# Gated scores in 32x32 tiles, keys times values in 64 columns, and finer waits, in a two-layer hybrid trunk

## The reference, cut to what matters

```
u = rms_norm(h) @ w_in            # split among four mixers
SSD and retention, 4 heads of 64: S_t = a_t S_{t-1} + k_t^T v_t,  o_t = q_t S_t       (a_t a scalar per head)
GLA, 4 heads, keys of 32:         S_t = diag(exp(g_t)) S_{t-1} + k_t^T v_t, o_t = q_t S_t
RG-LRU:                           h_t = a_t h_{t-1} + u_t, with gates sigmoid(x @ w_a), sigmoid(x @ w_x)
h += concat(y_ssd, y_ret, y_gla, y_lru) @ w_out
h += (silu(rms_norm(h) @ w_gate) * (rms_norm(h) @ w_up)) @ w_down     # 2816 wide
```

## Time and profile before

| what | value |
|---|---|
| median of 3 runs | 1399.87 us (1399.63 to 1401.17) |
| profiled execution | 1401.04 us |
| its span | 1399.0 us |
| PE busy | 1369.9 us, 98% of the span |
| PE weight loads | 1320.2 us, 94% |
| VectorE busy | 638.1 us, 46% |
| ScalarE busy | 492.9 us, 35% |
| GpSimd busy | 409.6 us, 29% |

### The profile page before, as it was taken

The page is one execution under the profiler, slowest core; times in us unless marked ns, Lnnn a source line. Parts: engine busy times, 40 slices in busy tenths (PEclk is TensorE's granted clock), DMA queues, the critical chain, the costliest instruction groups (busy, mean ns, idle before and its releaser), DMA issues.

```text
span 1399.0 us, 25881 instructions
## 1 busy us (share of the span) xinstructions
PE 1369.9 (98%) x11245; PEld 1320.2 (94%) x11245; DVE 638.1 (46%) x1234; ACT 492.9 (35%) x675; POOL 409.6 (29%) x204
## 2 busy tenths in 40 slices
PE   7999999999999999999999999999999999999996
PEld 7888888999999999999998798899999999999996
DVE  5844775553321443133657456646433123422434
ACT  6525354432221222122553364543322122222231
POOL 1100001434334443344400000024344334443341
PEclk9999999999999999999999999999999999999998
DMA  7745644222332223322466565422322232223321
GB/s 246 180 107 137 159 95 110 86 78 89 92 91 86 82 90 91 91 83 84 131 139 154 120 153 120 103 88 84 89 82 88 91 91 86 83 90 91 91 91 64
DMA packets 42065, 147.05 MB, mean 105 GB/s; under 512 B 5216, under 2 KB 6496, under 8 KB 41952
## 3 DMA queue, kind: packets, MB, share of 16 engines
q1 hardware_dynamic: 30672, 111.95, 25.4%
q0 software_dynamic: 6624, 24.12, 10.5%
q10 hardware_dynamic: 4656, 9.34, 2.1%
HBM read 137.34 MB, written 5.82 MB: 102 GB/s over the span
## 4 chain that ended last, share of the span: by engine, by line
PE 86%; DVE 8%; DVEq 2%; ACT 2%; issue 1%; DMA 1%; SPq 0%; ACTq 0%
PE bank L1264 77%; DVE ct L754 1%; PE bank L1212 1%; DVE lru_x L754 1%; PE bank L1394 1%; PE bank L1420 1%; PE bank L1509 1%; PE bank L1228 0%; DMA h<-x 0%; DVEq L753 0%; PE bank L1515 0%; PE bank L1223 0%; DVE sq_sum L688 0%; PE bank L1445 0%; DVE h L1203 0%
## 5 line engine op out<-in xcount | busy, mean ns | idle before, releaser
L1264 PE MATMUL bank<-xh,wh 128*128 128x272 f32 x2208 | 649.2, 294 | 8.0 <-DVE xl L709 7.7
L1264 PE MATMUL bank<-xh,wl 128*128 128x272 f32 x2208 | 641.5, 291 | 0.0
L1264 PE MATMUL bank<-xl,wh 128*128 128x272 f32 x2208 | 637.6, 289 | 0.0
L390 POOL TENSOR_TENSOR wl<-raw,wh 128x1024 fp32r<-128x1024 f32 x154 | 369.4, 2399 | 591.7 <-ACT wh L419 572.4
L1264 PEld LDWEIGHTS bank<-xh,wh 128*128 128x128 f32 x2208 | 418.4, 189 | 15.7 <-issue 13.4
L419 ACT ACTIVATE wh<-raw 128x1024 fp32r<-128x1024 f32 x199 | 210.2, 1056 | 611.4 <-PE bank L1264 611.4
L1264 PEld LDWEIGHTS bank<-xl,wh 128*128 128x128 f32 x2208 | 418.9, 190 | 1.4 <-issue 1.0
L1264 PEld LDWEIGHTS bank<-xh,wl 128*128 128x128 f32 x2208 | 417.7, 189 | 0.0
L1181 DVE TENSOR_TENSOR tz<-bank,rs_bcast 128x272 f32<-128x272 f32 x176 | 77.5, 442 | 293.3 <-PE bank L1264 289.3
L1161 DVE TENSOR_TENSOR h<-h,bank 128x272 f32<-128x272 f32 x128 | 55.4, 436 | 217.3 <-PE bank L1264 217.2
L396 POOL DMA_DIRECT2D wl<-weights x46 | 39.9, 868 | 371.7 <-ACT wl L418 371.7
(11 more groups left out here) (361 smaller groups left out, 1750.6 us busy)
## 6 DMA issues: line engine op xcount, KB each, us to landing
raw<-weights SPq DMA_DIRECT2D x202, 512.0 KB, 3.6
wl<-weights POOLq DMA_DIRECT2D x46, 512.0 KB, 6.9
h<-x SPq DMA_DIRECT2D x4, 544.0 KB, 6.0
y<-h SPq DMA_DIRECT2D x4, 544.0 KB, 2.7
rv<-rk ACTq DMA_DIRECT2D x8, 136.0 KB, 7.0
tz<-rq ACTq DMA_DIRECT2D x8, 136.0 KB, 4.6
S<-s_ssd ACTq DMA_DIRECT2D x2, 512.0 KB, 7.0
n_ssd<-Vx ACTq DMA_DIRECT2D x2, 512.0 KB, 3.2
```

The costliest lines, as they stand in the source:

```text
L390: nc.gpsimd.tensor_tensor(wl[:, s, :], raw[:, s, :], wh[:, s, :].bitcast(F32), ALU.subtract).then_inc(lo_done, 1)
L1264: ins = mm(bank_, wt[:, n % RING, w], xx[:, cols], start=(i == 0 and j == 0), stop=(i == len(ks) - 1 and j == 2))
```

## The change

Four things are changed; all else stays.

1. GLA's scores: `kz` and the product that filled it are gone. Each matmul takes 32 key rows of one head and 32 stationary columns (tile position (32 hd, 32 j)); head hd writes bank M[0], M[2], M[3] or M[4], and the order goes through diagonals, so that four neighbours differ in rows and columns. VectorE masks with four products. Since M[3] is now written here, `gla_a_` waits for `gla_s` of the chunk before, as `gla_b_` did.
2. Keys times values in SSD, GLA and retention: one matmul per group (per head in retention) with 64 stationary columns and only the values that belong to it. The states shrink from 256 to 128 columns, and so do the three state outputs.
3. `lru_gates`: the four matmuls into M[4] wait for the convolution alone, the gates of t = 0 for a new signal `ssd_read` (M[0] and M[1] read), those of t = 1 for `ssd_s`.
4. Order: in `ssd_a_` the decay matrix comes first, then transposes, scores and the 64-row decays last; in `ret_a_` all transposes come ahead of the scores.

```diff
+GLA_BANKS = (0, 2, 3, 4)
...
-        kz = sb("kz", [4, P])
+        st_stacks = sb("st_stacks", [4, P])
...
-        S_ssd, S_gla, S_ret = sb("S_ssd", [256]), sb("S_gla", [256]), sb("S_ret", [256])
+        S_ssd, S_gla, S_ret = sb("S_ssd", [P]), sb("S_gla", [P]), sb("S_ret", [P])
...
                     if c == SAMPLE:
-                        dve.drain()
+                        dve.drain().then_inc(ssd_read.sem, 1)
                         for r in range(2):
                             tt(S1[:, 512 * r:512 * r + 512], S1[:, 512 * r:512 * r + 512], M[2 + r][:], ALU.add)
                     else:
                         if c == 0:
-                            copy(S_ssd[:], M[2][:, 0:256])
+                            copy(S_ssd[:], M[2][:, 0:P])
...
-                    if c < SAMPLE:
-                        tt(kz[:], ge[:, 0, :].unsqueeze(1).to_broadcast([P, 4, n]), per_head(cst("gla_heads"), P, n),
-                           ALU.mult)
-                    else:
+                    if c == SAMPLE:
...
-                    tt(PT, M[0][:].rearrange("p (h i) -> p h i", h=4), cst("keep").unsqueeze(1).to_broadcast([n, 4, n]),
-                       ALU.mult)
+                    for hd in range(4):
+                        tt(PT[:, hd, :], M[GLA_BANKS[hd]][:, 0:n], cst("keep"), ALU.mult)
                     dve.drain().then_inc(gla_bin.sem, 1)
...
-                    for r in range(2):
-                        for g in range(2):
-                            mm(M[1][64 * g:64 * g + 64, r * P:r * P + P],
-                               exact("cum_head", P, 2 * g + r, 1).to_broadcast([P, 64]).bitcast(F32), cum.bitcast(F32), start=True, stop=True)
...
+                    for t in range(2):
+                        turn(M[2][:, P * (t + 1):P * (t + 2)], xbc[:, t, off:off + n])
+                    turn(M[1][:, 384:512], xbc[:, 2, off:off + n])
                     for g in range(2):
                         rows = slice(64 * g, 64 * g + 64)
                         mm(M[2 + g][:, 0:n], xbc[rows, 2, off:off + n], xbc[rows, 3, off:off + n], start=True, stop=True)
-                    for t in range(2):
-                        turn(M[2][:, P * (t + 1):P * (t + 2)], xbc[:, t, off:off + n])
-                    turn(M[1][:, 384:512], xbc[:, 2, off:off + n]).then_inc(ssd_a.sem, 1)
+                    for r in range(2):
+                        for g in range(2):
+                            ins = mm(M[1][64 * g:64 * g + 64, r * P:r * P + P],
+                               exact("cum_head", P, 2 * g + r, 1).to_broadcast([P, 64]).bitcast(F32), cum.bitcast(F32), start=True, stop=True)
+                    ins.then_inc(ssd_a.sem, 1)
...
-                    mm(M[2][:, 0:256], K[:, 0:P], Vd[:], start=True, stop=True).then_inc(ssd_b.sem, 1)
+                    for g in range(2):
+                        ins = mm(M[2][64 * g:64 * g + 64, 0:P], K[:, 64 * g:64 * g + 64], Vd[:, P * g:P * g + P],
+                                 start=True, stop=True)
+                    ins.then_inc(ssd_b.sem, 1)
...
                     pe.wait_ge(conv_done.sem, conv_done.at(layer, 6))
-                    pe.wait_ge(ssd_s.sem, ssd_s.at(layer, 5))
...
                     for t in range(2):
+                        if t == 0:
+                            pe.wait_ge(ssd_read.sem, ssd_read.at(layer, 1))
+                        else:
+                            pe.wait_ge(ssd_s.sem, ssd_s.at(layer, 5))
                         for i in range(2):
                             ins = mm(M[2 * t + i][:], gate(t, i), lru_x[:, t, 0:SEQ], start=True, stop=True)
                         ins.then_inc(lru_mm.sem, 1)
...
                         pe.wait_ge(gla_o.sem, gla_o.at(layer, c))
+                        pe.wait_ge(gla_s.sem, gla_s.at(layer, c))
...
-                    for hd in range(4):
-                        for j in range(4):
-                            mm(M[0][32 * j:32 * j + 32, hd * P:(hd + 1) * P], kz[:, hd, 32 * j:32 * j + 32],
-                               D[:, j, :], start=True, stop=True)
+                    for d in range(4):
+                        for hd in range(4):
+                            j, rows = (hd + d) % 4, slice(32 * hd, 32 * hd + 32)
+                            mm(M[GLA_BANKS[hd]][32 * j:32 * j + 32, 0:P], ge[rows, 0, 32 * j:32 * j + 32],
+                               D[rows, j, :], start=True, stop=True, tile_position=(32 * hd, 32 * j))
...
-                    mm(M[3][:, 0:256], K[:, 0:P], V[:], start=True, stop=True).then_inc(gla_b.sem, 1)
+                    for t in range(2):
+                        ins = mm(M[3][64 * t:64 * t + 64, 0:P], K[:, 64 * t:64 * t + 64], V[:, P * t:P * t + P],
+                                 start=True, stop=True)
+                    ins.then_inc(gla_b.sem, 1)
...
-                    for t in range(2):
-                        ins = mm(M[0][:, t * P:(t + 1) * P], K[:, t * P:(t + 1) * P], V[:, t * P:(t + 1) * P],
-                                 start=True, stop=True)
+                    for hd in range(4):
+                        t, e = hd // 2, hd % 2
+                        cols = slice(64 * hd, 64 * hd + 64)
+                        ins = mm(M[0][64 * e:64 * e + 64, 64 * t:64 * t + 64], K[:, cols], V[:, cols], start=True, stop=True)
                     ins.then_inc(ret_b.sem, 1)
```

More of the change, by code:

```diff
@@ L222, in trunk @@
         st_vx, st_wide = Vx[:, 1024:1536], Vx[:, 1536:2048]
-        st_k, st_q, st_kl, st_a = kz[:, 0, :], kz[:, 1, :], kz[:, 2, :], kz[:, 3, :]
+        st_k, st_q, st_kl, st_a = (st_stacks[:, i, :] for i in range(4))
         st_p, st_v, st_d, st_o = PT[:, 0, 0:NS], V[:, 0:64], V[:, 64:64 + NS], V[:, P:P + 64]
@@ L997, in gla_b_ @@
                     else:
-                        new = M[3][:, 0:256]
+                        new = M[3][:, 0:P]
                         if c == 0:
@@ L1057, in ret_b_ @@
                         for t in range(2):
[L1058 removed]
+                            cols = slice(64 * t, 64 * t + 64)
                             if c == 0:
@@ L1442, in gla_b_ @@
                         rows = slice(32 * hd, 32 * hd + 32)
-                        mm(M[2 - t][64 * e:64 * e + 64, 0:P], S_gla[rows, 64 * hd:64 * hd + 64],
+                        mm(M[2 - t][64 * e:64 * e + 64, 0:P], S_gla[rows, 64 * e:64 * e + 64],
                            qt[rows, (c + 1) % 2, 0, :], start=False, stop=True, tile_position=(32 * hd, 64 * e))
-                    mm(M[3][:, 0:256], K[:, 0:P], V[:], start=True, stop=True).then_inc(gla_b.sem, 1)
+                    for t in range(2):
+                        ins = mm(M[3][64 * t:64 * t + 64, 0:P], K[:, 64 * t:64 * t + 64], V[:, P * t:P * t + P],
+                                 start=True, stop=True)
+                    ins.then_inc(gla_b.sem, 1)
                 def ret_a_(c):
@@ L1468, in ret_a_ @@
                     for t in range(2):
+                        turn(M[3][:, 256 + t * P:256 + (t + 1) * P], rv[:, t, off:off + n])
+                    for t in range(2):
                         for e in range(2):
                             rows = slice(64 * e, 64 * e + 64)
-                            mm(M[e][0:n, t * P:t * P + n], rk[rows, t, off:off + n], rq[rows, t, off:off + n],
-                               start=True, stop=True)
-                    for t in range(2):
-                        ins = turn(M[3][:, 256 + t * P:256 + (t + 1) * P], rv[:, t, off:off + n])
+                            ins = mm(M[e][0:n, t * P:t * P + n], rk[rows, t, off:off + n], rq[rows, t, off:off + n],
+                                     start=True, stop=True)
                     ins.then_inc(ret_a.sem, 1)
@@ L1493, in ret_b_ @@
                         rows = slice(64 * e, 64 * e + 64)
-                        mm(M[3][64 * e:64 * e + 64, t * P:(t + 1) * P], S_ret[rows, 64 * hd:64 * hd + 64],
+                        mm(M[3][64 * e:64 * e + 64, t * P:(t + 1) * P], S_ret[rows, 64 * t:64 * t + 64],
                            qt[rows, c % 2, t, :], start=False, stop=True, skip_group_check=True)
-                    for t in range(2):
-                        ins = mm(M[0][:, t * P:(t + 1) * P], K[:, t * P:(t + 1) * P], V[:, t * P:(t + 1) * P],
-                                 start=True, stop=True)
+                    for hd in range(4):
+                        t, e = hd // 2, hd % 2
+                        cols = slice(64 * hd, 64 * hd + 64)
+                        ins = mm(M[0][64 * e:64 * e + 64, 64 * t:64 * t + 64], K[:, cols], V[:, cols], start=True, stop=True)
                     ins.then_inc(ret_b.sem, 1)
@@ L1800 @@
     conv_p, conv_s = conv[:, None, 0:3], conv[:, 3:].reshape(DEPTH, NSEQ, 3, 6 * P)
[L1801 to L1806 removed]
+    o_ssd = r["o_ssd"].reshape(DEPTH, 2, 64, 2, 64)
+    o_ret = r["o_ret"].reshape(DEPTH, 2, 64, 2, 64)
+    o_gla = r["o_gla"].reshape(DEPTH, 4, 32, 2, 64)
+    p_ssd = np.stack([o_ssd[:, h // 2, :, h % 2] for h in range(4)], axis=1)[:, None]
```

(2 more changed lines are left out.)

19 lines of the change are left out of this document (6 added, 13 removed).

## The result

The median after is 1394.21 us (1392.69 to 1401.40, 7 runs), beside 1400.82 us (1399.41 to 1406.38, 7 runs) of the kernel before on the same chip. The ratio is 0.9948, 95% interval 0.9923 to 0.9973. The profiled execution took 1394.02 us with a span of 1392.0 us, 7.0 us less than the one before. The kernel is faster, but the gain is half of the 13.1 us that were forecast: 6.6 by the medians, 8.8 once the time at the low clock is taken out. The median lies 0.3 us inside the upper end of the range.

A forecast was written before the change was run, and what follows sets the result against it. TensorE (PE) was taken to bound the kernel, with 86% of the chain. Savings of 4.2 + 1.6 + 1.0 + 1.2 + 3.0 + 1.7 + 0.4 = 13.1 from 1401.04 gave 1387.9 us, range 1383 to 1394.5.

The forecast's parts named there:

- Scores: GLA's scores in 32x32 tiles: 0.48 us instead of 1.01 per group, eight groups, 4.2 us saved, bounds 0 to 5.6.
- The first rival: GLA's scores: issue sets the pace, so the sixteen tiles gain nothing or little, 1392.1 us; chance 0.15.
- take turns: Slower rival at GLA's scores: the array does one record at a time, 3.5 us a group, 1412 us; chance 0.03.
- Keys times values: 64-column products: 1.6 us saved in SSD and GLA, bounds -0.6 to 3; 1.0 in retention, bounds 0 to 2.
- Reordered SSD groups: SSD stage a: three shape changes instead of four, 0.2 us for chunks 1 to 3, two layers: 1.2, bounds 0 to 2.
- The copy L900: VectorE's halved copy, ahead of L906 and the stall at L1350: 0.2 us in each of two layers, 0.4.
- The gates: Recurrence gates: PE's two stalls before L1391 vanish and nothing is late next, 3.0 us saved, bounds 2 to 3.
- The clock's 1.7: Layer 0's low clock after the gates' stall (L1394 5.19 against 3.50) counted as gained, bounds -1.7 to 3.4 us.
- the second rival: The clock's 1.7 us stays because the fall moves elsewhere: 1389.6 us; chance 0.25.
- The added wait: gla_a waits for gla_s of the chunk before: taken as 0, bounds 0 to 1 us per layer.
- four mask products: VectorE's mask product becomes four, 0.88 us instead of 0.69, inside 3 us of dense work: costs 0.
- the second stretch: From SSD's sampled chunk's state times queries to gla_b of chunk 0: 2.0 us saved per layer.

The follow-up runs named there:

- e11: The changed kernel with the old order of the groups in ssd_a_ and ret_a_ put back: 1394.62 us, ratio 0.9928.
- e5: The kernel before with only the finer waits of the recurrence's gates (ssd_read and three waits): 1402.09 us beside 1403.83, ratio 0.9988.
- e4: The changed kernel with ScalarE's four DMA issues after ssd_s moved behind gla_b of chunk 0: 1392.60 us, ratio 0.9933.
- e9: The changed kernel with the four DMA issues moved behind gla_b of chunk 1: 1389.03 us beside 1403.83, ratio 0.9886.
- e12: The kernel before with only the four DMA issues moved behind gla_b of chunk 1: 1400.28 us beside 1402.41, ratio 0.998.
- e1: The changed kernel measured again without any edit: 1394.75 us beside 1401.21, ratio 0.996.
- e2: The changed kernel with the recurrence's gates waiting for ssd_s as before, without the finer waits: 1395.34 us, ratio 0.9953.
- e7: The changed kernel with the scores in plain order, head by head instead of along diagonals: 1397.02 us.
- e3: The kernel before with only the 32-row scores (no kz, four banks, four mask products, the wait for gla_s): 1397.82 us, ratio 0.9961.
- e6: The changed kernel with the four DMA issues behind gla_b of chunk 0 and the gates' old wait: 1392.24 us, ratio 0.9912.

## Why the prediction was half right, step by step

**Scores: right, slightly better.** 0.53 a chunk was forecast, 0.58 measured (1.01 to 0.43), in all eight chunks. The pace was not the 0.015 per record that I took from L1308: the 32 starts stand 6.7 ns apart in runs of 16, as the trace records them, with 33 ns between the two sixteens, so 0.2 of the 0.43 is the change of shape behind them. L1308's 0.015 was an average that hid this: in the trace of before its eight starts are two fours, 6.7 ns apart within and 38 ns between, and L1420's are eight fours with 89 ns and more between. The first rival (nothing gained) did not happen, and those starts made it unlikely beforehand, though none stood closer than 38 ns to a fifth. The Trainium skill's rule that starts never come closer than about 25 ns (TensorE: Matmul & The Clock Gate, "Wait — 56ns, not 53.3ns?") would have made the group 0.80 at least. I took it to hold across tile positions, and there the trace disagrees, with 6.7 ns. The tiles did not take turns either. But only six of eight times 0.58 reached the end of the kernel: chunk 0's fell into the wait for K.

**Keys times values: the size was too large in SSD and GLA, too small in retention.** For SSD and GLA 0.10 a chunk was forecast, 0.06 measured: 0.66 to 0.60. The second dense start came after 0.23, as foreseen; the group itself takes 0.37 and not 0.33, which I had priced by L1515, whose 32x32 operands are small. GLA's chunk 0 gave 0.20, for a forecast of 0.22. For retention 1.0 was forecast in both layers together and 2.2 measured, by the table. The group saved 0.41, 0.26, 0.17 and 0.09 from start to start in chunks 0 to 3 (0.64, 0.64, 0.55, 0.47 before; 0.23, 0.38, 0.38, 0.38 after), or 0.9 a layer. I had counted three chunks only, and taken off 0.2 for leaving the 64-column shape, yet in the earlier trace rows the 64-column group L1515 already stands behind L1497: nothing new is left, and one change of shape goes. The last 0.2 a layer has no cause shown; it is within the error of that row.

**Reordered SSD groups: 0.2 a chunk forecast, 0.13 measured (e11).** Three changes of shape instead of four was right, and the two that the 64-column group had at the stage's start gave 0.20. But the change to 64 rows costs 0.14 behind the transposes, where it stands now, and had cost 0.09 behind the matrix. The delayed signal in chunk 0 takes 0.3 back over two layers.

**The copy L900: 0.4 forecast, nothing seen.** The wait for line 906 at the second SSD stage is 1.4 in two layers, and was 1.3. What the order and keys times values saved in three chunks, 3 x 0.19 = 0.57, is already the whole 0.5 of that stretch.

**The gates: this step failed.** The prediction said: "Nothing is late next: 3.0 us, bounds 2 to 3." It looked ahead on PE and on VectorE and not on ScalarE, the third engine that waits for `ssd_s`. The changed kernel's chain in order of time, layer 1, shows that engine from the signal to `gla_b`:

```profile
794.76 0.64 DVEq L906
...
795.42 0.35 ACTq L618
...
796.77 0.74 ACTq L621
...
797.61 1.06 ACT wl L419
...
799.63 1.28 ACT L500
...
804.21 1.28 ACT L506
...
810.41 0.17 ACT K L488
810.58 0.14 issue
810.72 0.66 PE bank L1443 x8
```

Four DMA issues take 2.2, splitting weights into their low and high parts 2.0, two loads of an activation table 1.28 each, with sigmoids and exponentials of the gates behind them, then another split, one more issue, and K: from `ssd_s` at 795.40 to PE's start 15.3 us, with no wait for another engine in the chain. In the kernel before the same row was there, and it was as good as late. ScalarE's timeline and the chain in order of time, kernel before, layer 1:

```profile
814.83 0.26 ACT L487 ACTIVATE K<-bank 128x128 f32<-128x128 f32 x1
```

```profile
815.14 0.10 issue
815.24 0.66 PE bank L1438 x8
```

K ended at 815.09 (814.83 + 0.26), and PE was through with its dense half at 815.14. In layer 0 of that trace K ended at 131.60 and PE came at 131.91, after a fall of the clock that cost PE's side 1.7 and an issue of 2.10 on ScalarE's. With so little slack (0.1 us in layer 1), nothing that shortens PE's side alone between `ssd_s` and `gla_b` can be gained: the stall's 1.5, the scores of chunk 0 (0.58), a layer. Only what makes `ssd_s` earlier counts, and that was kz's 0.7. e5 shows the loss alone, e4 and e9 give it back by making the row shorter, e12 shows that the row cost nothing before. No row of the trace of before names this wait, for it was never the last; the timeline of ScalarE in that stretch would have told it.

**The clock's 1.7: not gained; the second rival came true.** The gates' fall (at 116.9 us) is gone, as foreseen. But the profiled execution has falls at 171.7 and 195.6 instead, behind the groups of twenty small matmuls. The chain in order of time, for the second:

```profile
192.61 2.09 PE bank L1547 x20
194.70 4.74 PE bank L1261 x24
```

4.74 for a half that takes 3.02 at full clock: 1.7, and the same behind the other fall (4.73). And the fall behind the stall did not always go: it can move with it. e1's trace, the same kernel, has it right behind the new stall for K, the chain in order of time:

```profile
128.46 0.66 PE bank L1443 x8
...
129.34 4.73 PE bank L1261 x24
```

The traces of e2 and e11 have a fall at the same place, and e5's in layer 1. In all twelve traces PE stands for 1.5 to 1.9 us at the gates or at `gla_b` of chunk 0 in sixteen layers, and in six of them a fall begins 1.0 to 1.7 us after PE has started again; in the eight layers without such a stall none does there. So the prediction's link between stall and fall held, but the stall was still in the kernel. Counted over all runs the kernel before spends 29.7 us at the low level and the one after 31.9, with a spread (standard error about 1 and 2.6) that can't tell them apart.

**Other steps.** The added wait for `gla_s` appears in no list of waits: 0, as forecast. The four mask products take 0.88 instead of 0.69, hidden. In the second stretch, then, 2.0 a layer was forecast and 0.7 came; SSD lost 0.6, retention won 0.6. Over both layers: 11.4 - 2.6 - 1.2 + 1.2 = 8.8. The forecast's own sum misses by the gates' stall and the clock; the others cancel, which is luck. That the median still fell inside the range is luck too: the range's upper part was there for the sixteen tiles, the clock and the added wait, of which only the clock's 1.7 came, and not for a stall that moves; the repeat (e1) lies just outside.

## What to carry to other kernels

Before a stall of one engine is booked as a gain, follow every engine that waits for the same signal to the next point where they meet, and write down each one's slack there: a list of waits shows only who was last, never who was 0.1 us behind. Issues and stores at the head of a long row can be moved for nothing, but it pays only once the row is the late one. Cost a change of tile shape at both ends of the group, and from start to start: the chain's pieces put modelled ends between the groups, and would have told here that the dense half behind got 0.21 slower, where the starts say 0.08 faster. And look at the single starts of a dense group before its mean is used as a pace.

## What the runs showed of the hardware that I had not expected

- Matmuls with 32x32 positions start 6.7 ns apart, sixteen in a row, whether neighbours differ in row group and bank or share them (e7). In the kernel before, L1308, L1375, L1379 and L1420 start 6.7 ns apart too, but only two or four in a row, with 38 to 154 ns between.
- Whether the group ahead has 64 or 128 stationary columns makes no difference of more than 0.05 us to the 24 starts of a dense half at full clock (2.96 to 3.01 from the first to the last). Behind groups with 256 and 512 moving columns they take 3.07 and 3.3, since the second start comes later (0.31 and 0.53 behind the first, not 0.23).
- A DMA issue among the four behind `ssd_s` takes 0.35 to 0.8 us in most traces, but single ones took 2.10 in the kernel before, 1.85 in e2, 1.75 in e3, and 1.0 to 2.0 in e4, e6 and e12, in either layer. Where the row on ScalarE was the late one, the stretch to `gla_b` grew by as much (1.1 for 1.85 - 0.74 in e2, 1.0 in e3). The cause is open.
- Of the 48 falls of the clock ahead of the last norm, in twelve traces, 33 come behind the groups of twenty matmuls with few columns (about 2 us of PE's time), 9 behind the two groups of ten of a norm, and 6 behind a stall of 1.5 to 1.9 us. They differ between executions of one kernel and carry most of the scatter of its times: before, 1397.8 to 1410.4 us over all its runs. What decides whether one happens stays open.
